# Paged attention of a hybrid decoder step: the two key halves as two column tiles of TensorE

## What is computed

```python
def _attend_paged(q_nope, q_pe, ckv_new, kpe_new, w_uk, w_uv, pool_ckv, pool_kpe, layer, page_table):
    q_lat = einsum('bthn,chn->bhtc', q_nope, w_uk) * MLA_SCALE     # 16 heads x 4 tokens, 512 latent
    q_rot = swapaxes(q_pe, 1, 2) * MLA_SCALE                       # 64 rotary
    ...
    def online(carry, ck, kp, mask):
        s = einsum('bhtc,bkc->bhtk', q_lat, ck) + einsum('bhtr,bkr->bhtk', q_rot, kp)
        ...                                  # running max, exp, running sum, acc += pr @ ck
    carry, _ = lax.scan(page_step, init, page_table.T)             # 8 pages of 128 keys
    _, l, acc = online(carry, ckv_new, kpe_new, causal)            # 4 new keys, causal
    o = einsum('bhtc,chv->bthv', acc / l[..., None], w_uv)
```

## Time and profile before

| what | value |
|---|---|
| time, median of 3 runs | 3621.45 us (3621.26 to 3621.45) |
| profiled execution, span from first to last instruction | 3618.2 us |
| PE busy | 3264.6 us, 90% of the span |
| DVE busy | 1618.7 us, 45% |
| ACT busy | 1148.5 us, 32% |
| POOL busy | 134.7 us, 4% |
| DMA | 456.20 MB, mean 126 GB/s |

### The profile page before, as it was taken

How to read it: one execution, slowest core, us unless ns; L and a number is a source line. 1 busy time by engine, 2 the same in 40 slices (tenths; PEclk the granted TensorE clock), 3 DMA queues, 4 the chain that set the end, 5 groups by cost and what they waited for, 6 DMA issues and landing times.

```text
span 3618.2 us, 54195 instructions
## 1 busy us (share of the span) xinstructions
PE 3264.6 (90%) x22046; PEld 3005.8 (83%) x22046; DVE 1618.7 (45%) x1742; ACT 1148.5 (32%) x1129; POOL 134.7 (4%) x147
## 2 busy tenths in 40 slices
PE   5999659979999999999887877888999999999987
PEld 4998537669999999999887854334999999999987
DVE  4655345645444444444555322111554444444444
ACT  2333411113333333343342223221333333423333
POOL 2000000002000000000010000000100000000002
PEclk9999856679999999999998866998999999999998
DMA  4545200115455555555443211214555555555542
GB/s 127 162 129 154 92 12 25 49 48 166 151 164 166 168 164 162 163 165 168 130 137 105 68 53 30 76 52 114 154 153 163 163 164 166 168 163 162 164 138 85
DMA packets 454679, 456.20 MB, mean 126 GB/s; under 512 B 22217, under 2 KB 440074, under 8 KB 453981
## 3 DMA queue, kind: packets, MB, share of 16 engines
q1 hardware_dynamic: 454608, 455.23, 41.1%
HBM read 446.97 MB, written 8.22 MB: 126 GB/s over the span
## 4 chain that ended last, share of the span: by engine, by line
PE 84%; DVE 7%; ACT 4%; issue 3%; DMA 1%; SPq 0%; POOL 0%; ACTq 0%; DVEq 0%; POOLq 0%
PE ps L1154 81%; PE ps L1161 2%; ACT Wh L1184 2%; DVE Wl L1508 1%; DVE acc L1605 1%; DVE Al L1531 0%; DVE TT L1781 0%; DMA W<-in_w_in_a 0%; DVE kpT L2007 0%; SPq L466 0%; ACT sc L1427 0%; DMA gw<-in_lru_wi 0%; DVE hT L1535 0%; POOL ssacc L2061 0%; ACT ckT L1454 0%
## 5 line engine op out<-in xcount | busy, mean ns | idle before, releaser
L1508 DVE TENSOR_TENSOR Wl<-W,Wh 128x2048 fp32r<-128x2048 f32 (+2 forms) x408 | 910.3, 2233 | 1114.9 <-ACT Wh L1184 1099.1
L1184 ACT ACTIVATE Wh<-W 128x2048 fp32r<-128x2048 f32 (+2 forms) x408 | 758.1, 1860 | 1227.8 <-PE ps L1154 1208.5
L1154 PE MATMUL ps<-Ah,Wh 128*128 128x288 f32 x3344 | 991.4, 296 | 33.3 <-DVE Wl L1508 27.9
L1154 PE MATMUL ps<-Al,Wh 128*128 128x288 f32 x3344 | 990.0, 296 | 0.0
L1154 PE MATMUL ps<-Ah,Wl 128*128 128x288 f32 x3344 | 990.0, 296 | 0.0
L1154 PE MATMUL ps<-Bh,Wh 128*128 128x288 f32 x2704 | 799.2, 296 | 11.5 <-DVE Bl L1822 10.3
L1154 PE MATMUL ps<-Bh,Wl 128*128 128x288 f32 x2704 | 799.9, 296 | 0.0
L1154 PE MATMUL ps<-Bl,Wh 128*128 128x288 f32 x2704 | 799.9, 296 | 0.0
L1154 PEld LDWEIGHTS ps<-Ah,Wh 128*128 128x128 f32 x3344 | 629.9, 188 | 38.2 <-DVE Wl L1508 27.8
L1154 PEld LDWEIGHTS ps<-Al,Wh 128*128 128x128 f32 x3344 | 630.5, 189 | 0.5
L1154 PEld LDWEIGHTS ps<-Ah,Wl 128*128 128x128 f32 x3344 | 629.8, 188 | 0.3
(11 more groups left out here) (392 smaller groups left out, 2679.7 us busy)
## 6 DMA issues: line engine op xcount, KB each, us to landing
W<-in_w_up SPq DMA_DIRECT2D x128, 1024.0 KB, 5.6
W<-in_w_down SPq DMA_DIRECT2D x128, 1024.0 KB, 5.3
W<-in_w_in_a SPq DMA_DIRECT2D x48, 1024.0 KB, 5.4
W<-in_w_ple_gate SPq DMA_DIRECT2D x32, 1024.0 KB, 5.3
W<-in_w_out_a SPq DMA_DIRECT2D x16, 1024.0 KB, 5.4
CK<-in_cache_ckv SPq DMA_DIRECT2D x64, 256.0 KB, 2.5
W<-in_w_o_c SPq DMA_DIRECT2D x16, 1024.0 KB, 5.4
W<-in_w_ukv SPq DMA_DIRECT2D x12, 1024.0 KB, 5.6
```

The costliest lines, as they stand in the source:

```text
L1154: return m.nc.tensor.matmul(out, w, x, start=start, stop=stop)
L1184: last = A(x, w, ACT.Copy)
L1508: last = TT(low, w, f(high), SUB)
```

## The change

Keys 0 to 511 keep output partitions 0 to 63, keys 512 to 1023 now go to partitions 64 to 127 of the same bank, and the matmuls of the two halves alternate. The softmax then works on 128 partitions by 512 columns; since the maximum, the sum and the inverse belong to rows of both halves, DVE copies one column between the partition halves where they meet (four copies more, and `reduce_max` and `reduce_sum` over three columns in place of two-operand operations). The probabilities are transposed in four pieces of 128x128. The value matmuls of pages 0 to 3 go to partitions 0 to 63 and those of pages 4 to 7 to partitions 64 to 127 of bank 7, again alternating, after the one of the new keys. The four transposes of the result become four plain matmuls with `fold`, two identities of 64 one above the other, which add the halves. `fold` is made once by DVE.

```diff
@@ scores (PE)
-        for o, ck, kp in ((ps[0:64, 0, :], m.ckT[:, :, 0:512], m.kpT[0:64, 0:512]),
-                          (ps[0:64, 1, :], m.ckT[:, :, 512:1024], m.kpT[0:64, 512:1024]),
-                          (ps[0:64, 2, 0:NS], m.c[:, 4:8, SEQ:NT], m.kpe[0:64, SEQ:NT])):
-            for k in range(4):
-                mm(o, ql[k], ck[:, k, :], k == 0, False)
-            last = mm(o, qr, kp, False, True)
-        last.then_inc(m.sa_s, 1)
+        for k in range(4):
+            for half in range(2):
+                mm(ps[64 * half:64 * half + 64, 0, :], ql[k], m.ckT[:, k, 512 * half:512 * half + 512], k == 0, False)
+        for half in range(2):
+            mm(ps[64 * half:64 * half + 64, 0, :], qr, m.kpT[0:64, 512 * half:512 * half + 512], False, True)
+        for k in range(4):
+            mm(ps[0:64, 2, 0:NS], ql[k], m.c[:, 4 + k, SEQ:NT], k == 0, False)
+        mm(ps[0:64, 2, 0:NS], qr, m.kpe[0:64, SEQ:NT], False, True).then_inc(m.sa_s, 1)
@@ values (PE)
-        mm(ps[:, 3, 0:64], m.sc8[0:64, 0:128], m.ident[0:64, 0:64], True, True)
-        for n in range(1, NPG):
-            tr(ps[:, 3, 64 * n:64 * n + 64], m.sc8[0:64, 128 * n:128 * n + 128], 128)
-        tr(ps[0:NS, 6, 0:64], m.sc8[0:64, PAST:PAST + NS], 64).then_inc(m.sa_pt, 1)
+        for n in range(NPG // 2):
+            tr(ps[:, 3, 128 * n:128 * n + 128], m.sc8[:, 128 * n:128 * n + 128], 128)
+        tr(ps[0:NS, 6, 0:64], m.sc8[0:64, PAST // 2:PAST // 2 + NS], 64).then_inc(m.sa_pt, 1)
...
-        for n in range(NPG):
-            mm(ps[0:64, 7, :], m.PT[:, n, :], m.CK[i][:, n, :], n == 0, False)
-        mm(ps[0:64, 7, :], m.PTn[0:NS, :], m.ckn[0:NS, :], False, True).then_inc(m.spv_mm, 1)
+        mm(ps[0:64, 7, :], m.PTn[0:NS, :], m.ckn[0:NS, :], True, False)
+        for n in range(NPG // 2):
+            for half in range(2):
+                last = mm(ps[64 * half:64 * half + 64, 7, :], m.PT[:, n, half, :],
+                          m.CK[i][:, 4 * half + n, :], n == 0 and half == 1, n == NPG // 2 - 1)
+        last.then_inc(m.spv_mm, 1)
         pe.wait_ge(m.sa_av, 4 * t + (i + 1))
-        mm(ps[:, 6, 128:192], m.acc64[0:64, 0:128], m.ident[0:64, 0:64], True, True)
-        for k in range(1, 4):
-            last = tr(ps[:, 6, 128 + 64 * k:192 + 64 * k], m.acc64[0:64, 128 * k:128 * k + 128], 64)
+        for k in range(4):
+            last = mm(ps[:, 6, 128 + 64 * k:192 + 64 * k], m.acc2[:, 128 * k:128 * k + 128], m.fold[:], True, True)
@@ ACT
-        A(m.acc64[0:64, :], ps[0:64, 7, :], ACT.Copy, scale=m.mx8[0:64, i % 2, 6:7]).then_inc(m.sa_av, 1)
+        A(m.acc2[:], ps[:, 7, :], ACT.Copy, scale=m.mx8[:, i % 2, 9:10]).then_inc(m.sa_av, 1)
...
-            A(m.sc8[0:64, 0:PAST], ps[0:64, 0:2, :].rearrange("p b n -> p (b n)"), ACT.Exp, bias=w[:, 2:3],
-              scale=MLA_SCALE, accum_out=w[:, 3:4])
+            A(m.sc8[:, 0:PAST // 2], ps[:, 0, :], ACT.Exp, bias=w[:, 4:5], scale=MLA_SCALE, accum_out=w[:, 5:6])
@@ DVE
+    TT(m.fold[:], m.ident[:, 0:64], m.ident[:, 64:128], ADD).then_inc(m.fold_set, 1)
     dve.sem_inc(m.sa_acc, 1)
...
-            V.reduce_max(w[:, 0:1], ps[0:64, 0:2, :].rearrange("p b n -> p (b n)"), AX.X)
+            V.reduce_max(w[:, 0:1], ps[:, 0, :], AX.X)
             own.after(TT(m.nsc[0:64, :], ps[0:64, 2, 0:NS], new[0:64, ds(t * -16 + (NS - TS - 4 * i), NS)], ADD))
-            own.after(V.reduce_max(w[:, 1:2], m.nsc[0:64, :], AX.X))
-            own.after(TT(w[:, 0:1], w[:, 0:1], w[:, 1:2], MAX))
-            TS2(w[:, 2:3], w[:, 0:1], -MLA_SCALE, None, MUL).then_inc(m.sa_m, 1)
+            V.tensor_copy(low[:, 1:2], high[:, 0:1])
+            own.after(V.reduce_max(low[:, 2:3], m.nsc[0:64, :], AX.X))
+            own.after(V.reduce_max(low[:, 3:4], low[:, 0:3], AX.X))
+            own.after(TS2(low[:, 4:5], low[:, 3:4], -MLA_SCALE, None, MUL))
+            V.tensor_copy(high[:, 4:5], low[:, 4:5]).then_inc(m.sa_m, 1)
             dve.wait_ge(m.sa_e, 4 * t + (i + 1))
-            own.after(TT(w[:, 5:6], w[:, 3:4], w[:, 4:5], ADD))
-            V.reciprocal(w[:, 6:7], w[:, 5:6]).then_inc(m.sa_r, 1)
+            own.after(V.tensor_copy(low[:, 7:8], high[:, 5:6]))
+            own.after(V.reduce_sum(low[:, 8:9], low[:, 5:8], AX.X))
+            own.after(V.reciprocal(low[:, 9:10], low[:, 8:9]))
+            V.tensor_copy(high[:, 9:10], low[:, 9:10]).then_inc(m.sa_r, 1)
```

More of the change, by code:

```diff
@@ L253, in semaphores @@
     m.r_done = sem("r_done")
+    m.fold_set = sem("fold_set")
     m.sa_r, m.sa_av, m.sa_at = sems("sa_r sa_av sa_at")
@@ L384, in memory @@
     m.mx2 = at("mx2", o + 6144, [4, 4])
-    m.PT = at("PT", o, [NPG, 64])
+    m.PT = at("PT", o, [NPG // 2, 2, 64])
     m.PTn = at("PTn", o + 2048, [64])
     m.nsc = at("nsc", o + 2304, [NS])
-    m.mx8 = at("mx8", o + 2432, [2, 8])
+    m.mx8 = at("mx8", o + 2432, [2, 12])
     m.ckn = at("ckn", o + 2560, [512])
-    m.acc64 = at("acc64", o + 4608, [512])
+    m.acc2 = at("acc2", o + 4608, [512])
+    m.fold = at("fold", o + 6656, [64])
     o += 8 * T1
@@ L399, in memory @@
     m.sv = at("sv", o, [HM * VH])
-    m.sc8 = at("sc8", oR, [PAST + NS])
+    m.sc8 = at("sc8", oR, [PAST // 2 + NS])
     m.csq = at("csq", oA, [8, NT])
@@ L1096, in values @@
         pe.wait_ge(m.sa_e, 4 * t + (i + 1))
-        mm(ps[:, 3, 0:64], m.sc8[0:64, 0:128], m.ident[0:64, 0:64], True, True)
-        for n in range(1, NPG):
-            tr(ps[:, 3, 64 * n:64 * n + 64], m.sc8[0:64, 128 * n:128 * n + 128], 128)
-        tr(ps[0:NS, 6, 0:64], m.sc8[0:64, PAST:PAST + NS], 64).then_inc(m.sa_pt, 1)
+        for n in range(NPG // 2):
+            tr(ps[:, 3, 128 * n:128 * n + 128], m.sc8[:, 128 * n:128 * n + 128], 128)
+        tr(ps[0:NS, 6, 0:64], m.sc8[0:64, PAST // 2:PAST // 2 + NS], 64).then_inc(m.sa_pt, 1)
         pe.wait_ge(m.sa_ptc, 4 * t + (i + 1))
         pe.wait_ge(m.sa_nt, 4 * t + (i + 1))
-        for n in range(NPG):
-            mm(ps[0:64, 7, :], m.PT[:, n, :], m.CK[i][:, n, :], n == 0, False)
-        mm(ps[0:64, 7, :], m.PTn[0:NS, :], m.ckn[0:NS, :], False, True).then_inc(m.spv_mm, 1)
+        mm(ps[0:64, 7, :], m.PTn[0:NS, :], m.ckn[0:NS, :], True, False)
[4 more added lines that the diff above has]
+        last.then_inc(m.spv_mm, 1)
         pe.wait_ge(m.sa_av, 4 * t + (i + 1))
-        mm(ps[:, 6, 128:192], m.acc64[0:64, 0:128], m.ident[0:64, 0:64], True, True)
-        for k in range(1, 4):
-            last = tr(ps[:, 6, 128 + 64 * k:192 + 64 * k], m.acc64[0:64, 128 * k:128 * k + 128], 64)
+        for k in range(4):
+            last = mm(ps[:, 6, 128 + 64 * k:192 + 64 * k], m.acc2[:, 128 * k:128 * k + 128], m.fold[:], True, True)
         last.then_inc(m.sa_at, 1)
     pe.wait_ge(m.ckn_done, BASE["ckn_done"] + 1)
+    pe.wait_ge(m.fold_set, 1)
     with pe.Fori(0, 2) as t:
@@ L1442, in probs_t @@
         act.wait_ge(m.sa_pt, 4 * t + (i + 1))
-        A(m.PT[:].rearrange("p n r -> p (n r)"), ps[:, 3, :], ACT.Copy).then_inc(m.sa_ptc, 1)
+        A(m.PT[:].rearrange("p n g r -> p (n g r)"), ps[:, 3, :], ACT.Copy).then_inc(m.sa_ptc, 1)
     def values(t, i):
@@ L1458, in scalar_program @@
             act.wait_ge(m.sa_m, 4 * t + (i + 1))
-            w = m.mx8[0:64, i % 2, :]
-            A(m.sc8[0:64, 0:PAST], ps[0:64, 0:2, :].rearrange("p b n -> p (b n)"), ACT.Exp, bias=w[:, 2:3],
-              scale=MLA_SCALE, accum_out=w[:, 3:4])
-            A(m.sc8[0:64, PAST:], m.nsc[0:64, :], ACT.Exp, bias=w[:, 2:3], scale=MLA_SCALE, accum_out=w[:, 4:5]
-              ).then_inc(m.sa_e, 1)
+            w = m.mx8[:, i % 2, :]
+            A(m.sc8[:, 0:PAST // 2], ps[:, 0, :], ACT.Exp, bias=w[:, 4:5], scale=MLA_SCALE, accum_out=w[:, 5:6])
+            A(m.sc8[0:64, PAST // 2:], m.nsc[0:64, :], ACT.Exp, bias=w[0:64, 4:5], scale=MLA_SCALE,
+              accum_out=w[0:64, 6:7]).then_inc(m.sa_e, 1)
             if i:
@@ L2010, in samples @@
             dve.wait_ge(m.sa_s, 4 * t + (i + 1))
-            w = m.mx8[0:64, i % 2, :]
-            V.reduce_max(w[:, 0:1], ps[0:64, 0:2, :].rearrange("p b n -> p (b n)"), AX.X)
+            w = m.mx8[:, i % 2, :]
+            low, high = w[0:64], w[64:128]
+            V.reduce_max(w[:, 0:1], ps[:, 0, :], AX.X)
             own.after(TT(m.nsc[0:64, :], ps[0:64, 2, 0:NS], new[0:64, ds(t * -16 + (NS - TS - 4 * i), NS)], ADD))
-            own.after(V.reduce_max(w[:, 1:2], m.nsc[0:64, :], AX.X))
-            own.after(TT(w[:, 0:1], w[:, 0:1], w[:, 1:2], MAX))
-            TS2(w[:, 2:3], w[:, 0:1], -MLA_SCALE, None, MUL).then_inc(m.sa_m, 1)
+            V.tensor_copy(low[:, 1:2], high[:, 0:1])
[3 more added lines that the diff above has]
+            V.tensor_copy(high[:, 4:5], low[:, 4:5]).then_inc(m.sa_m, 1)
             dve.wait_ge(m.sa_e, 4 * t + (i + 1))
-            own.after(TT(w[:, 5:6], w[:, 3:4], w[:, 4:5], ADD))
-            V.reciprocal(w[:, 6:7], w[:, 5:6]).then_inc(m.sa_r, 1)
+            own.after(V.tensor_copy(low[:, 7:8], high[:, 5:6]))
+            own.after(V.reduce_sum(low[:, 8:9], low[:, 5:8], AX.X))
```

(4 more changed lines are left out.)

## The result

The changed kernel takes 3553.64 us (median of 4 runs, 3551.0 to 3557.01) against 3621.36 us (3605.79 to 3621.45): a ratio of 0.9825, 95% interval 0.9806 to 0.9845, so 56 to 70 us faster. Forecast were 3581 us in a range of 3560 to 3622: the sign was right, the size was not.

The account below looks back on a forecast made before the run. PE's matmuls were taken to bound the kernel. Savings of 52.2 us (whole overlap) or 35.9 (loads in the open) gave a middle of 44, less 4 for the clock: 3621.45 - 40 = 3581 us, range 3560 to 3622.

Parts of the forecast that it names:

- scores: Score matmuls on PE: 9.12 us per sample would shrink by 3.70 with whole overlap, 2.61 with loads in the open.
- values: Value matmuls for cached pages on PE: 6.87 us per sample would shrink by 3.01, or 2.06 with loads in the open.
- transposes of the probabilities: PE, before ACT's copy: five new pieces replace nine short ones, 0.97 to 0.80 us, 0.17 saved per sample.
- fold: PE, result transposes: four plain matmuls, eight records, take 1.09 to 1.23 us, taken as 1.16; 0.42 lost per sample.
- softmax of two samples: DVE and ACT: 0.23 us saved, counting only in two samples with nothing beside their softmax, 0.5 us for the kernel.
- clock, outside the values: PE's clock, forecast only as a whole: more lowered stretches cost 4 us; bounds 14 us lost to 10 gained.
- low end of part 1: Score matmuls: halves overlap wholly, 12 slots of 0.429 us plus 0.27, 5.42 us, a saving of 3.70 per sample.
- rivals without overlap: Score and value matmuls: halves run one after the other as now, about 0.7 us saved, 3621 us; chance 0.15.
- with a stop at each change of half: Rival for score and value matmuls: each change of column half stops PE, 15 x 0.135 us per sample, 3637 us; chance 0.12.
- part 1: The score matmuls on PE, 20 records per sample: 9.12 us now, saving between 0.27 and 3.70.
- the middle between loads hidden and loads in the open: Score and value matmuls: between 52.2 us saved with weight loads beside running matmuls and 35.9 with loads in front; 44 taken.
- the whole overlap: Score and value matmuls run fully side by side on both halves: 6.46 us per sample, 52.2 us in all.

Follow-up runs that it names:

- runs by half: Two runs, each the changed kernel with all half 0 matmuls before half 1: latent scores 3570.27 us (0.9878), values 3563.81 us (0.9864).
- two by two: The changed kernel with score and value matmuls alternating between halves in groups of two matmuls, four records: 3555.67 us (0.9824).
- scores by half: The changed kernel with the latent score matmuls of half 0 all before those of half 1, values still alternating: 3570.27 us (0.9878).
- the last run: The changed kernel with four column tiles behind the loop, bank 1 as third page-transpose buffer, second half of rotary transposes in bank 7: 3535.33 us (0.978).

## Why the prediction was wrong in size

Measured per term, summed over the eight samples of the profiled loops, saved (+) or lost (-):

| term | forecast, us | measured, us |
|---|---|---|
| scores | 25.2 (20.9 to 29.6) | 36.3 (9.12 to 4.59 per sample) |
| values | 20.3 (16.5 to 24.1) | 27.5 (8.08 to 4.65 per sample at full clock) |
| transposes of the probabilities | 1.4 | 1.0 (0.97 to 0.85) |
| fold | -3.4 | -3.9 (0.74 to 1.23) |
| softmax of two samples | 0.5 | 0.4 (4.25 to 4.04 of PE's wait) |
| clock, outside the values | -4 for all | +3.7 (page transposes, 66.7 to 63.0) |
| sum | 40 | 65.0 |

- **The bound was right:** PE's long matmuls, and what they lost came off the end. Nothing was late next: the chain has no DMA in the loop and no softmax in front of a value matmul.
- **The overlap was right** in its mechanism: the halves stream side by side, and their loads lie beside running matmuls, as in the low end of part 1. The rivals without overlap and with a stop at each change of half fell; a change of half costs nothing that the trace shows (16 records in 8 slots and 0.14 us). The Trainium skill (TensorEngine Tiling (Array Packing), Key Properties) says that different tiles load and multiply in parallel, and the pairs of loads agree.
- **The step that failed** is in part 1: "I take it that matmuls start in program order ... The first and the last stand alone." That made 12 and 9 slots; the trace shows 10 and 8, three slots or 1.29 us per sample, 10.3 us. The runs by half (12 slots) and two by two (8) show in its place that PE starts a record of the free half ahead of up to three waiting ones. So no record stands alone. The Trainium skill (TensorE: Matmul & The Clock Gate, The mechanism) states that matmuls start and end strictly in program order; the 12 slots in the run of scores by half disagree, and the measurement decides.
- **A term mis-sized:** I took the middle between loads hidden and loads in the open. The earlier trace rows showed them hidden on one half, and the trace after shows two loads in 0.17 us inside each slot of 0.43; the middle cost 8.1 us of the forecast.
- **The clock** was set down as 4 us lost. The value stages lost as much as before, six times 1.7 us against four times 1.7 and once 3.3, and the page transposes met fewer lowered stretches. At full clock these take 7.05 to 7.18 us per sample in both kernels, and what is above that goes with the granted clock, as in the second sample, before and after:

```profile
2268.89:2279.11 10.22, 8.57 (x40) 7.51 (x41) 1.36 (x2) 4.76 (x8) 0.00 (x0) 0.57 0.24 59
2259.45:2267.93 8.48, 6.69 (x41) 5.69 (x41) 1.36 (x2) 4.67 (x8) 0.00 (x0) 0.80 0.66 175
```

From 4 us lost to 3.7 gained is 7.7 us off. I found no cause for which stretch is lowered: two profiles of the changed kernel agree in it, and small edits move it.

- **The fold** came out at the upper of its two bounds, 1.23 us, reckoned from the pair of records in the old fold. The softmax came out as forecast (maximum 0.68 us, exponential 0.69).

8.1 + 10.3 + 7.7 less about 1 for fold, transposes and softmax are the 25 us between 40 and 65. My range rested on the slot count too: its low end was the whole overlap at 12 and 9 slots with 10 us for the clock, and the slots alone would have put it 10 us lower. What moved the clock was not tested and stays open.

## What to carry to other kernels

In this kernel float32 matmuls with 64 columns of weights, one after the other on the same output partitions, were halved in time by placing them in turn on both partition halves (16 records, 6.99 to 3.58 us), and those with 32 columns nearly quartered (14.18 to 3.70 us). Other types were not tried. Look for it where such records step by their full streaming time. Keep partners close in the program (here within three waiting records), and count the joining of the halves (0.5 us per sample here). Then look at what the shorter stage leaves: sparse transposes, a late weight load, and a clock that took back half of what the page transposes gained in the last run.

## What was not expected of the hardware

- A record of the free column half started ahead of three waiting records of the busy one, not ahead of four (12 slots by half, 8 two by two). Why it stops there is open.
- Two float32 streams of 512 columns on both halves cost no more than one: 0.43 us per pair. Four tiles of 32 columns too: 128 records in 3.43 us, 0.107 per four.
- Two column halves with fewer shared rows (64 rotary rows) pair as well: four records in 2294.04 - 2293.03 = 1.01 us, where two took 1.00.
